# Two more gates of each feed-forward block in side-by-side form, with two low parts and one sum on GpSimd

## The reference

```python
x = layer_norm(ALPHA * x + 0.5 * swiglu(x, ffn1...), ln1_g, ln1_b)
h = x @ w_in          # stick-breaking heads and chunked heads, then w_out
x = layer_norm(ALPHA * x + mixed @ w_out, ln2_g, ln2_b)
x = layer_norm(ALPHA * x + 0.5 * swiglu(x, ffn2...), ln3_g, ln3_b)

def swiglu(x, w_gate, w_up, w_down):
    return (silu(x @ w_gate) * (x @ w_up)) @ w_down   # 1024 -> 2816 -> 1024
```

## Time and profile before

| | us |
|---|---|
| median of three runs | 960.83 |
| the profiled execution | 960.22 |
| its span, from the first to the last instruction | 958.2 |
| TensorE (PE) busy | 947.7 |
| VectorE (DVE) busy | 854.6 |
| ScalarE (ACT) busy | 632.0 |
| GpSimd (POOL) busy | 21.5 |

### The profile page before, as it was taken

One profiled execution on the slowest core, in us unless ns is written; L12 is line 12 of the kernel. 1 busy time (PEld: TensorE's weight loads), 2 busy tenths in 40 slices (PEclk: granted clock), 3 DMA queues, 4 the chain that ended last, 5 costly groups with the idle time before them and its releaser, 6 DMA issues.

```text
span 958.2 us, 15318 instructions
## 1 busy us (share of the span) xinstructions
PE 947.7 (99%) x5418; PEld 817.7 (85%) x5418; DVE 854.6 (89%) x1121; ACT 632.0 (66%) x771; POOL 21.5 (2%) x53
## 2 busy tenths in 40 slices
PE   9999999999999999999999999999999999999996
PEld 9978888888788988888998888898887889888885
DVE  6999998966899999998999999988578989999986
ACT  6666665568884667675566767655678755767653
POOL 0000000001100000000000000000010000000000
PEclk9999999999999999999999999999999999999999
DMA  8576644572344655555636575554633445645554
GB/s 318 209 264 235 246 175 178 218 263 89 132 152 156 220 204 213 183 212 195 220 132 215 182 302 180 219 167 185 220 136 122 166 161 211 224 177 220 175 186 155
DMA packets 34653, 187.28 MB, mean 195 GB/s; under 512 B 3888, under 2 KB 3888, under 8 KB 19504
## 3 DMA queue, kind: packets, MB, share of 16 engines
q1 hardware_dynamic: 33120, 177.22, 51.4%
q0 software_dynamic: 1488, 9.45, 2.7%
HBM read 185.61 MB, written 1.05 MB: 195 GB/s over the span
## 4 chain that ended last, share of the span: by engine, by line
PE 93%; DVE 6%; issue 1%; ACT 0%; DVEq 0%; POOL 0%; POOLq 0%
PE bank L1594 68%; PE bank L1450 8%; PE bank L1452 8%; PE bank L1451 8%; PE bank L1513 1%; DVE xn L1000 1%; PE bank L1825 1%; DVE xn L1019 1%; DVE w_lo L947 1%; DVE w_lo L966 0%; DVE w_lo L904 0%; DVE qT L1034 0%; DVE stick_t L926 0%; DVE h_lo L1140 0%; DVE w_lo L954 0%
## 5 line engine op out<-in xcount | busy, mean ns | idle before, releaser
L1594 PE MATMUL bank<-xT,w_hi 128*128 128x512 f32 (+1 forms) x1248 | 397.2, 387 | 0.0
L1594 PEld LDWEIGHTS bank<-xT,w_lo 128*128 128x128 f32 x1200 | 223.2, 188 | 49.6
L1594 PE MATMUL bank<-xT,w_lo 128*128 128x256 f32 x1200 | 234.6, 278 | 0.0
L505 ACT ACTIVATE w_hi<-raw 128x2048 fp32r<-128x2048 f32 x116 | 221.7, 1911 | 1.6 <-DMA raw<-stream 1.6
L1594 PEld LDWEIGHTS bank<-xT,w_hi 128*128 128x128 f32 x1248 | 198.0, 189 | 6.0 <-issue 0.8
L904 DVE TENSOR_TENSOR w_lo<-raw,w_hi 128x2048 fp32r<-128x2048 f32 x54 | 123.5, 2287 | 10.1 <-ACT w_hi L505 9.9
L646 ACT ACTIVATE ez<-bank 128x512 f32<-128x512 f32 x64 | 38.4, 600 | 103.3 <-PE bank L1594 103.3
L1594 PE MATMUL bank<-w_hi,h_hi 128*128 128x512 f32 x252 | 98.5, 391 | 1.4 <-DVE h_lo L1140 1.4
L1594 PE MATMUL bank<-w_lo,h_hi 128*128 128x512 f32 x252 | 98.6, 391 | 0.0
L1594 PE MATMUL bank<-w_hi,h_lo 128*128 128x512 f32 x252 | 98.4, 391 | 0.0
L1450 PE MATMUL bank<-xT,w_hi 128*128 128x256 f32 x304 | 86.2, 284 | 0.0
(11 more groups left out here) (188 smaller groups left out, 1572.7 us busy)
## 6 DMA issues: line engine op xcount, KB each, us to landing
raw<-stream SPq DMA_DIRECT2D x110, 1024.0 KB, 4.8
raw<-stream SPq DMA_DIRECT2D x110, 512.0 KB, 4.5
lnp<-ln_gb POOLq DMA_DIRECT2D x6, 1024.0 KB, 5.3
band<-rel_band POOLq DMA_DIRECT2D x2, 1024.0 KB, 9.7
xn<-x POOLq DMA_DIRECT2D x1, 1024.0 KB, 6.9
out<-xn SPq DMA_DIRECT2D x4, 256.0 KB, 2.0
qT<-first SPq DMA_DIRECT2D x2, 384.0 KB, 4.0
kT<-first SPq DMA_DIRECT2D x2, 384.0 KB, 5.4
```

The source lines that it names most:

```text
L505: nc.scalar.activation(w_hi[:, at(slot if into is None else into)], raw[:, slot, :], ACT.Copy).then_inc(hi_ready, 1)
L1594: return nc.tensor.matmul(o, w, x, start=start, stop=stop, skip_group_check=True)
```

## The change

The first gate in the steps (`gate(1)`) and the last (`gate(SF)`) of each FFN are made by `gate_half`, as the others are. That has parts on every engine:

```diff
 # GpSimd, a new function, at the start of each FFN's turn
+            def first_step(l, f):
+                base = FFN_BASE[f]
+                wait_alone(hi_ready, l * UNITS + (base + 7))
+                wait_alone(lo_ready, split(l, base + 5))
+                for c, done in enumerate((up_lo_first, lo_ready)):
+                    raw_c, hi_c, lo_c = (t.rearrange("p (k d) -> p k d", k=KC)[:, :, c * P:(c + 1) * P]
+                                         for t in (raw[:, 0, :], w_hi[:, at(0)], w_lo[:, at(0)]))
+                    nc.gpsimd.tensor_tensor(lo_c, raw_c, hi_c.bitcast(F32), ALU.subtract).then_inc(done, 1)
+                wait_alone(gate_copied, 2 * wide_gate(l, f, 1) + 2)
+                nc.gpsimd.tensor_tensor(gate_sums[:, :, 0:T], gate_sums[:, :, 0:T], gate_sums[:, :, T:2 * T],
+                                        ALU.add).then_inc(gate_summed, 1)
 # ScalarE
-                differences(1)
-                up_hi(2)
-                last_of_h_and_parts(1)
-                act.wait_ge(hf_done, it(l, f, 1) + 1)
-                silu(2, 5)
-                next_gate(1)
-                copy_up(2, 0)
-                next_pure(2)
-                copy_up(2, 1)
-                with act.Fori(2, SF - 1) as j:
+                with act.Fori(1, SF - 1) as j:
                     step(j)
                 step(SF - 1, more=False)
                 split_hi(l, base + 3 * SF + 3, 0, first[0] + 1 + SF)
+                copy_gate(SF, 0)
...
-                silu(FP - 1, 3 * SF + 2)
+                copy_gate(SF, 1)
                 split_hi(l, base + 3 * SF + 5, 2, first[2] + 1 + SF)
+                silu_sums(SF)
 # VectorE: step 1
-                    if r < 0:
-                        low_h(j + 1)
-                        split_up_lo(l, base + 3 * j + 6, 0)
-                        split_up_lo(l, base + 3 * j + 6, 1)
-                        split_differences_lo(l, f, j + 1)
-                    else:
-                        split_differences_lo(l, f, j + 1)
-                        low_h(j + 1)
-                        split_up_lo(l, base + 3 * j + 6, 0)
-                        split_up_lo(l, base + 3 * j + 6, 1)
+                    split_differences_lo(l, f, j + 1)
+                    low_h(j + 1)
...
+                dve.wait_ge(lo_ready, split(l, base + 6))
                 split_last_parts_lo(l, base + 7)
 # VectorE: the end of an FFN
                 up_sum(SF, 1)
+                split_lo(l, base + 3 * SF + 3, 0)
                 gather(l, f, 2)
-                split_lo(l, base + 3 * SF + 3, 0)
...
                 gather(l, f, 3)
+                gate_sum(SF)
                 split_lo(l, base + 3 * SF + 4, 1)
                 split_lo(l, base + 3 * SF + 5, 2)
 # TensorE
-                gate(1)
-                step(1, first=True)
+                product(6, True, parts=(0,))
+                pe.wait_ge(silu_done, it(l, f, 1) + 1)
+                gate_half(1, 0)
+                rest(start=True)
+                gate_half(1, 1)
+                step(1)
...
-                rest(stop=True)
-
-                gate(SF)
+                gate_half(SF, 0)
+                rest(stop=True)
+                gate_half(SF, 1)
```

More of the change, by code:

```diff
@@ L321, in wide_gate @@
         def wide_gate(l, f, j):
-            return (2 * l + f) * (SF - 2) + (j - 2)
+            return (2 * l + f) * SF + (j - 1)
         def wide(l, f, j):
@@ L466, in causal @@
                                         channel_multiplier=-1).then_inc(done, 1)
[L469 to L472, removed]
-            for l in range(DEPTH):
+            def first_step(l, f):
[9 more added lines that the diff above has]
+                                        ALU.add).then_inc(gate_summed, 1)
+            for l in range(DEPTH):
+                first_step(l, 0)
+                if l == 0:
+                    pool.wait_ge(raw_ready[1], 64)
+                    pool.dma_start(xn[:, :, :], x_in.rearrange("(b p) d -> p b d", p=P)).then_inc(x_loaded, 16)
+                    pool.wait_ge(x_loaded, 16)
+                    pool.sem_inc(xn_done, 4)
                 wait_alone(lo_ready, split(l, 15))
@@ L490, in _ @@
                 load_lnp(l, 2)
+                first_step(l, 1)
         @block.scalar
@@ L1179, in ffn @@
                     if j == 0 and r < 0:
-                        gated(j + 1, 3 * j + 3, bank[6])
+                        gated(j + 1, 3 * j + 3, bank[7])
                         split_lo(l, base + 3 * j + 5, 2)
@@ L1614, in ffn @@
                 base = FFN_BASE[f]
[L1616 to L1619, removed]
                 def gate_half(j, c):
@@ L1628, in gate_half, with up_half @@
                     wide_half(bank[0], 2, c).then_inc(unit_used if c else gate_first, 1)
-                def up_half(j, c, first=False):
+                def up_half(j, c):
                     if c == 0:
[L1633 to L1636, removed]
+                        pe.wait_ge(gate_copied, 2 * wide_gate(l, f, j) + 2)
                         pe.wait_ge(up_lo_first, (2 * l + f) * (SF - 1) + j)
@@ L1653, in product, with rest, step @@
                         last.then_inc(signal, 1)
-                def rest(stop=False):
+                def rest(start=False, stop=False):
                     product(6, signal=m_done if stop else None, parts=(1, 2))
-                    product(4, signal=unit_used)
-                def step(j, stop=False, first=False):
+                    if start:
+                        pe.wait_ge(hf_done, it(l, f, 1) + 1)
+                    product(4, start, unit_used)
+                def step(j, stop=False):
                     n = seven_step(l, f, j)
@@ L1666, in step @@
                     product(1, signal=finished)
-                    up_half(j, 0, first)
+                    up_half(j, 0)
                     product(3, signal=None if stop else pure_used)
@@ L1684, in ffn @@
                     first_three(l)
-                    u1, order = 6, (2, 1, 3, 5, 7, 4, 6)
+                    pe.wait_ge(hf_done, 1)
                 else:
@@ L1696, in ffn @@
                     columns(l, base + 2, 2, bank[0], (1,))
-                    u1, order = 7, (2, 1, 3, 5, 7, 6, 4)
-                columns(l, base + 3, 0, bank[u1])
+                columns(l, base + 3, 0, bank[7])
                 n = seven_step(l, f, 0)
                 pe.wait_ge(hlo_done, it(l, f, 0) + 1)
[L1701 to L1710, removed]
-                gate(1)
-                step(1, first=True)
+                pe.wait_ge(lo_part, 2 * n + 1)
+                product(2, True)
+                product(1, True)
+                product(3, True, pure_used)
+                pe.wait_ge(lo_part, 2 * n + 2)
+                product(5, True)
+                product(7, True, parts_used)
+                pe.wait_ge(lo_ready, split(l, base + 4))
+                product(6, True, parts=(0,))
[4 more added lines that the diff above has]
+                step(1)
                 with pe.Fori(2, SF - 1) as j:
```

## The result

The changed kernel takes **984.09 us** (median of four runs, 983.04 to 984.88) against 961.27 for the kernel before (960.59 to 961.72): a ratio of 1.024, 95% interval 1.0227 to 1.0252. It is slower, as forecast, but by 22.8 us and not by 12.6; the time lies above the range. The profiled execution has 983.9 us, span 982.2.

The account below looks back on a forecast made before the run. TensorE's pace bounds the kernel, plus every delay by a late VectorE (slack 0.34 us). 2.84 + 3 x 2.5 + 3 x 0.8 - 0.18 = 12.6 us on the median 960.83 gives 973.4 us; range 961.5 to 982.

Parts of the forecast that it names:

- The stop at the port: Step 1: GpSimd reads and VectorE's two-input SBUF operations stop each other; difference 2.0 us, sum 1.1; VectorE's list 2.84 longer.
- The place: TensorE waits at step 2 for the low hidden part: 2.84 us in the first FFN, 2.5 in each later one.
- the clock: Behind stalls: the 1.4 us stall left it full; 3 us stalls at 1.2 GHz would lie in the upper end.
- reordering: Around the gates: the rest of `product` and `rest` changes order only; no cost in the sum.
- The ends: `hl_lo` comes 0.8 us later at three FFN ends, so TensorE loses 0.8 each; the last FFN loses nothing.
- The gates: Two side-by-side gates in each of four FFNs gain TensorE 0.18 us each, 1.4 at most; only 0.18 entered the sum.
- Cheap and free GpSimd: Rivals in step 1: operations at 1.08 and 0.63 us, 964.1 us, chance 0.10; GpSimd unhindered beside VectorE, 958.0 us, 0.10.
- Starved GpSimd: Rival, step 1: GpSimd's sum gets no turn, silu and up copies wait, 5.4 us per FFN; 984.6 us, chance 0.05.

Follow-up runs that it names:

- Experiments 4 to 6: Kernel before plus three unneeded two-input GpSimd subtractions per FFN, 978.56 us; plus six memsets instead, 960.49; the change with memsets for GpSimd's operations, 961.67.
- experiment 7: The change with six matmuls of no use in each FFN ahead of TensorE's wait in step 1: 976.50 us.
- Experiments 1 and 2: The change with all its arithmetic on VectorE, 969.38 us; the same with the up unit's first low half ahead of `low_h`, 964.91.
- experiment 3: The change with the two differences back on VectorE and only the first wide gate's sum on GpSimd: 974.09 us.

## Why the prediction was right in direction and too small in size

**The stop at the port was right, and so was its price.** I took 2.0 us for a difference and 1.1 for the sum; the stretched rows say 2.14 to 2.21 and 1.07. VectorE's list grows by 5.42 - 2.26 = 3.16 where I had 2.84. Experiments 4 to 6 show that the reads do it: two-input operations of no use stretch VectorE, memsets don't, and the change without reads loses 1.8 us. The Trainium skill's "SBUF — State Buffer" (section "Who interferes with whom") says both, that a VectorE instruction with two SBUF inputs contends with a GpSimd instruction that reads SBUF and not with one that only writes it; this case's rows agree, 2.2 us against nothing.

**The place was wrong, and hardly mattered in three FFNs.** I had TensorE wait at step 2 and left open on which side of `low_h` GpSimd gets its turn. It gets two ahead of it, so the stall stands ahead of step 1. There 2.21 + 2.14 meet a slack of 333.67 - 332.07 = 1.60, and VectorE begins its stretch with 0.41 less lead on TensorE (5.08 us from L955 to step 1's due time of 340.50, before 5.49 from L947; 0.18 of it is the shorter gate, the rest I didn't trace): 4.35 - 1.60 + 0.41 = 3.16, measured 3.23. In the first FFN it did matter: both differences and the sum, 2.21 + 2.07 + 1.06, and now the down tile's differences too (1.2 us), stand ahead of `low_h`. `low_h` ends 6.26 us later than before (44.56 instead of 38.30), of which 1.16 was slack. 5.57 us are lost at step 1, and only the 1.52 of step 2 come back: 4.05 instead of 2.84. The four waits together are 13.8 instead of 10.3.

**The step that failed is the clock.** The prediction put it aside in one line: the stall of 1.4 us had left the clock at full, and slower running would lie in the upper end. (For the full clock it named rows 1, in which a fall of 3.4 us can hide; the row of before above bears it out.) It had itself forecast stalls of 2.5 to 2.8 us, about which that row says nothing, and gave the term no price. Behind stalls of 5.57, 3.23, 3.54 and 3.01 us the clock was half for 6.8, 3.4, 6.8 and 3.4 us, which cost 8.7 us; experiment 7 takes it away and gains 7.6 (6.8 from its own kernel before). This one term is three quarters of the 11.4 us between the two sums; without it the sum would have been some 976, inside the range. The Trainium skill's "TensorE: Matmul & The Clock Gate" (section "HAM oscillation — how this bites in real kernels") prices such time at its length times 1 - 1.2/2.4. By that an estimate from the four stretches is 20.4 x 0.5 = 10.2 us; the trace has less, since TensorE stood still for part of them.

**An idle that wasn't counted.** Moving product 4 behind the first half of the gate was called reordering. Experiments 1 and 2 show that it makes VectorE wait 0.91 us for the high hidden part, 4.5 us of the all-VectorE form, 1.7 of it the half clock. In the change itself GpSimd's turns lie over that idle.

**The ends** were forecast at 0.8 each and are 0.96; the layer norm's 0.5 to 1 us behind one of them was missed. **The gates** gain 0.19 each, 1.5 us against the 1.4 of the prediction, none of it visible; I had only the last FFN's in the sum.

**The rivals.** Cheap and free GpSimd fall with the rows of L476 and with experiment 4. *Starved GpSimd*, at 984.6, comes nearest to the time, within 0.5 us, and that is chance, for its mechanism is absent: GpSimd got every second turn, its sum came at once, and no up copy waited behind a silu.

## What to carry to other kernels

Before work is handed from VectorE to GpSimd, ask whether both read SBUF at that time: if so it isn't moved but lengthened, here 2.2 us of standing still for 1.13 us of work saved; the memsets, which only write, were free. A forecast stall of TensorE of some microseconds needs a second term, the pace behind it, and matmuls of no use in the stall are a cheap test for it. And an order in which a product is moved back by a few microseconds is a change of its own: follow who waits for that product.

## What the runs showed that I had not expected

- In all the rows read here the two engines alternate when both have such work: one VectorE operation, one of GpSimd, whatever their lengths. A 0.28 us `h_sums` row waits as long as a 1.2 us row does (2.49 and 3.43).
- The clock's fall doesn't follow from a stall's length alone. Behind stalls of 2.0 to 2.1 us it fell once in four (experiment 3), twice in four (experiment 4) and once in one (experiment 1); behind those of 1.4 us never; behind one of 3.16 us ahead of the matmuls of no use in the first FFN of experiment 7 it stayed full. The fall in experiment 3, behind the second FFN's stall of 2.01 us; the stretch begins 0.6 us before it, so it has 0.59 and not half:

```profile
354.90:358.30 3.40, 3.40 (x13) 2.85 (x12) 3.33 (x6) 0.63 (x1) 0.00 (x0) 0.59 0.73 264
```

  So in a kernel with stalls of this size the same change may or may not pay for the clock; what decides between them stays open.
